# A three-part block kernel: the first expert's weights are loaded during the mixing of attention rows, empty places are left out of the gathers, and two waits of the combination move to their first use

## The chip, the cores and the metric

The kernel runs on one core of one Trainium2 chip. The metric is the device time of one execution in microseconds (us). The kernel before was run three times; a separate execution was profiled, and every row below comes from that one.

## What is computed

The program is two network blocks in float32. The first has two layers (DEPTH = 2). Each layer projects its tokens to queries, keys and values, does attention, mixes the result through an output matrix, applies a layer norm, and then sends each token to a mixture of 32 experts. Layer 0 works on 768 tokens (512 latent, 256 context), layer 1 on the 512 latent ones. The part that matters here, in short (4 groups of 8 experts, 1024 to 512 to 1024 columns):

```python
g_idx = argmax(h @ w_group + b_group)
top_v, top_i = lax.top_k(e_logits[group], 2)
weights = softmax(g_logits)[g_idx] * softmax(top_v)
y_e = (silu(x_e @ w1[e]) * (x_e @ w3[e])) @ w2[e]
out = sum over the token's two experts of weight * y_e
h = layer_norm(ALPHA * h + mods * out, ln_g, ln_b)
```

So layer 0 has 2 x 768 = 1536 assignments of a token to an expert, layer 1 has 1024. All 32 experts' weights are read in each layer: w1, w3 and w2 take 2.10 MB each, 6.29 MB an expert and 201.3 MB a layer. The second block (a recurrent, a convolutional and a dilated branch, gates and a feed-forward part) follows; only its first step, which also finishes the first block, is touched.

## The kernel before

The program is a list of phases, each closed by a barrier of all engines (`program`, L2844). For each layer: `projection_phase`, `attention_phase` (L747), `routing_phase` (L1328), `expert_phase` (L1548). Then `combine_turn_phase` (L1699) and the second block.

**Attention.** qT, kT and V lie in SBUF from the projection to the end of the attention. After the last score tile is weighed (L983), TensorE mixes the rows tile by tile through wout (L998), VectorE makes the layer norm (L1255 to L1273), and the router's logits are made (L1014). SyncE (SP) issues all plain transfers, in the order in which they are written: in this stretch it stores the rows f and h of each tile (L889, L891) and fetches a later tile's (L895).

**Routing.** The routing phase turns the logits into tables. The rows of an expert are cut into units of 32 places (UNIT), at least one unit for each expert. `unit_end` says where each expert's units end, `gather_at` which row of f belongs in each place, `scatter_at` where its result goes. An empty place has row 0 in `gather_at` (L1540), and a number beyond the end, BIG, in `scatter_at` (L1541 to L1545). The experts are put in a sequence: experts 0, 1 and 2 first (EARLY_SLOTS = 3), then the others by their number of rows, in the pattern middle, next below the middle, largest, smallest (L1389 to L1393), so that large and small ones alternate. SP loads the weights of the three early experts in this phase (L1400).

**Experts.** There are four slots for weights (SLOTS = 4), and the load for place i of the sequence goes to slot i modulo 4. The fourth slot's memory is free only once the routing is over. The SP program is this loop (L1588); `load_gate` fetches w1 and w3 in two transfers (L1319), `load_down` w2 in one (L1325):

```python
for i in range(EARLY_SLOTS, NE):
    e = sp.value_load(unit_end[0:1, NE + 1 + i:NE + 2 + i], min_val=0, max_val=NE - 1)
    done = end_of(sp, i - SLOTS) if i >= SLOTS else None
    if i >= SLOTS:
        sp.wait_ge(hidden, done)
    load_gate(sp, g, l, i, e)
    if i >= SLOTS:
        sp.wait_ge(multiplied, done)
    load_down(sp, g, l, i, e)
```

TensorE walks through the sequence. For a unit it multiplies the turned rows xT by w1 and w3 (64 matmuls, L1648), then, after ScalarE's silu (L1667) and VectorE's product and turn (L1684, L1686), by w2 (32 matmuls, L1655). GpSimd (POOL) gathers the rows of the units ahead by an indirect transfer of 128 x 1 KB (L1607), and scatters each result (L1612). The signal `hidden` counts units after L1648, `multiplied` after L1655.

The units of the 32 places of the sequence follow from the inputs. They were counted with the reference's own routing, and agree with the unit boundaries that the trace shows. Layer 0 (64 units): 1 1 1 2 1 7 1 2 1 5 1 2 1 4 1 2 1 4 1 3 1 3 1 3 1 3 1 3 1 3 1 1. Layer 1 (54 units): 3 1 4 1 1 4 1 1 1 3 1 2 1 3 1 2 1 3 1 2 1 2 1 2 1 2 1 2 1 2 1 1. Expert 3 has 5 rows (one unit) in layer 0, and 107 rows (four units) in layer 1.

**Combination.** `combine_turn_phase` works on four tiles of rows. SP fetches, in this order (L1729 to L1740): three 0.52 MB pieces of tile 0 and the gate row; three pieces of tile 1, a 2.10 MB weight block (`load_weights` 1, L1924), the layer norm's two rows (lrow, 0.52 MB each) and gcol; three pieces of tile 2 and another 2.10 MB block; then tile 3. ScalarE weighs the first piece of a tile (L1775), VectorE adds the second and the residual (L1818 to L1825), ScalarE takes the root and norms (L1779, L1781), and VectorE applies lrow (`complete`, L1835). Two waits stand ahead of the loops: ScalarE's for gcol (L1798) and VectorE's for lrow (L1849).

## Time and profile before

| | |
|---|---|
| Median of three runs | 3466.02 us (3466.01 to 3468.59) |
| The profiled execution's own time | 3463.67 us |
| Its span, first to last instruction | 3461.9 us |
| Mean granted TensorE clock | 0.944 |
| Busy: PE, DVE, ACT, POOL | 2905.0, 1047.6, 757.6, 511.8 us |
| Moved by transfers | 684.84 MB |

The busy time of an engine is its instructions' time in the span; "PEclk" is the granted clock as a share of full speed. The page also cuts the span into 40 slices of 86.5 us, with the transfer engines' busy share and GB/s in each. Times inside the trace are counted from the span's start. The layers' expert stretches are the two runs of slices with 422 or 423 GB/s.

### The profile page before, as it was taken

What the parts mean: (1) busy time and instruction counts of PE and PEld (TensorE: products, weight loads), DVE (VectorE), ACT (ScalarE), POOL (GpSimd) and SP (SyncE); (2) the same over time, 40 slices, a digit from 0 to 9 for tenths busy, and PEclk for the clock granted to TensorE, in tenths of its full rate; (3) what the DMA queues carried; (4) which work ended last, traced back from release to release, by engine and by line L of the source; (5) the groups of instructions that cost most, each with busy time, mean ns of one, the idle gap of its engine ahead of it and who ended that gap; (6) DMA issues with size and microseconds to landing.
All of it is one profiled execution on the core that took longest, in us unless ns stands there. A gap on an engine that the chain in (4) does not pass through costs nothing. (4 is left out here: it accounts for less than half of the span.)

```text
span 3461.9 us, 50715 instructions
## 1 busy us (share of the span) xinstructions
PE 2905.0 (84%) x20913; PEld 1617.1 (47%) x20913; DVE 1047.6 (30%) x2201; ACT 757.6 (22%) x1483; POOL 511.8 (15%) x628
## 2 busy tenths in 40 slices
PE   7998888588776698895866652999999999999999
PEld 4555654355444345653534331444444554544444
DVE  3425856311111344754111113443211231211101
ACT  2224641111111323620111112311112220210000
POOL 0003720233332001611322220000000000000000
PEclk8999998799999799996989986999999999999999
DMA  7833002999998552007999996112222112322237
GB/s 296 313 130 114 1 19 106 423 422 423 422 423 368 209 122 96 1 37 294 422 422 422 423 423 244 61 50 81 73 73 73 49 65 79 89 84 87 97 116 260
DMA packets 188525, 684.84 MB, mean 198 GB/s; under 512 B 51438, under 2 KB 92842, under 8 KB 163782
## 3 DMA queue, kind: packets, MB, share of 16 engines
q1 hardware_dynamic: 176550, 655.66, 48.8%
q0 software_dynamic: 11808, 26.78, 2.0%
q8 instruction: 127, 2.08, 0.2%
q14 instruction: 40, 0.33, 0.0%
HBM read 653.89 MB, written 33.98 MB: 199 GB/s over the span
## 5 line engine op out<-in xcount | busy, mean ns | idle before, releaser
L1648 PE MATMUL pH<-w,xT 128*32 128x256 f32 x7552 | 473.5, 406 | 146.4 <-DMA w<-in_moe_w 123.1
L1648 PEld LDWEIGHTS pH<-w,xT 128*32 128x32 f32 x7552 | 295.9, 117 | 305.4 <-issue 179.8
L1655 PE MATMUL pY<-w,hT 128*32 128x256 f32 x3776 | 229.1, 382 | 151.6 <-DVE hT L1686 136.5
L2713 PE MATMUL banks<-hT,wf 128*128 128x512 f32 (+2 forms) x768 | 303.2, 557 | 3.3 <-ACT hT L2770 2.8
L1684 DVE TENSOR_TENSOR hh<-hs,pH 128x128 f32<-128x128 f32 x118 | 33.9, 287 | 807.7 <-ACT hs L1667 807.7
L923 POOL TENSOR_SCALAR E<-E,st 128x768 f32<-128x768 f32 (+3 forms) x80 | 168.3, 2104 | 660.4 <-DVE st L1173 659.8
L1655 PEld LDWEIGHTS pY<-w,hT 128*32 128x32 f32 x3776 | 131.7, 109 | 248.7 <-issue 181.6
L2713 PEld LDWEIGHTS banks<-hT,wf 128*128 128x128 f32 x768 | 140.8, 190 | 164.6 <-issue 154.9
L416 PE MATMUL pa<-aT,w 128*128 128x512 f32 x416 | 206.7, 602 | 1.3 <-DVE aT L680 1.3
L2459 PE MATMUL pa<-hT,ring 128*128 128x512 f32 x384 | 167.8, 592 | 0.0
L2364 PE MATMUL pa<-hT,ring 128*128 128x512 f32 x384 | 165.0, 592 | 1.3 <-PEq L91 1.3
L968 PE MATMUL pT<-ident,E 128*128 128x128 f32 x672 | 112.7, 287 | 55.0 <-ACT PT L1078 31.3
L2752 PE MATMUL banks<-ring,aT 128*128 128x512 f32 x352 | 151.2, 592 | 0.0
L2011 PE MATMUL pa<-hT,ring 128*128 128x512 f32 x320 | 144.2, 607 | 0.0
L998 PE MATMUL pS<-wout,oT 128*128 128x512 f32 x320 | 141.4, 594 | 0.8 <-issue 0.8
L1607 POOL DMA_INDIRECT xg<-f,at_x x124 | 130.2, 1050 | 62.0 <-POOL at_x L1606 58.8
L1612 POOL DMA_INDIRECT y<-y,at_y x122 | 126.1, 1033 | 60.8 <-POOL at_y L1631 59.6
L1667 ACT ACTIVATE hs<-pH 128x128 f32<-128x128 f32 x118 | 32.8, 278 | 466.8 <-PE pH L1648 466.8
L1670 ACT ACTIVATE y<-pY 128x256 f32<-128x256 f32 x118 | 45.4, 385 | 354.8 <-PE pY L1655 354.8
L968 PEld LDWEIGHTS pT<-ident,E 128*128 128x128 f32 x672 | 71.4, 142 | 99.8 <-issue 47.2
L2364 PEld LDWEIGHTS pa<-hT,ring 128*128 128x128 f32 x384 | 72.9, 190 | 93.4 <-issue 93.4
L937 PE MATMUL pS<-kT,qT 64*128 64x256 f32 (+2 forms) x608 | 109.5, 477 | 8.4 <-ACT E L1067 4.9
(468 smaller groups left out, 3653.9 us busy)
## 6 DMA issues: line engine op xcount, KB each, us to landing
w<-in_moe_w SPq DMA_DIRECT2D x192, 2048.0 KB
mw<-in_mod_w SPq DMA_DIRECT2D x24, 2048.0 KB, 16.6
ring<-in_w_ff_down SPq DMA_DIRECT2D x33, 1024.0 KB, 4.8
ring<-in_w_in SPq DMA_DIRECT2D x15, 2048.0 KB, 8.1
ring<-in_w_gate SPq DMA_DIRECT2D x6, 2048.0 KB, 8.6
wf<-in_w_ff_gate SPq DMA_DIRECT2D x11, 1024.0 KB, 5.7
wf<-in_w_ff_up SPq DMA_DIRECT2D x11, 1024.0 KB, 8.1
w<-in_ab_w_in SPq DMA_DIRECT2D x6, 1024.0 KB, 6.5
```

The source lines that it names most:

```text
L416: last = pe.matmul(pa[n % 2][:, 0:512], w[:, i % SLOTS_W, k, tile(c)], aT[:, k, 0:512], start=(k == 0), stop=(k == C - 1))
L923: pool.tensor_scalar(e, e, st[:, u % 4, 6 + b:7 + b], None, ALU.mult).then_inc(readyP, 1)
L968: last = pe.transpose(pT[:, tile(j)], E[:, u % NB, b, tile(i)], ident[:])
L998: last = pe.matmul(pS[n % 2][:, half * 512:(half + 1) * 512], oT[:, k, tile(n)], wout[:, k, half * 512:(half + 1) * 512], start=(k == 4), ...
L1607: pool.indirect_dma_start(out=xg[:, b], out_offset=None, in_=x_rows, in_offset=bass.IndirectOffsetOnAxis(ap=at_x[:, b:b + 1], axis=0), bou ...
L1648: last = pe.matmul(pH[strip(s), 0:2 * P].rearrange("p (j n) -> p j n", j=2), xT[:, k, :], slot_of(g, "w13", b)[:, :, k, s * P:(s + 1) * P] ...
L1655: last = pe.matmul(pY[strip(s), 0:YW], hT[:, k, :], slot_of(g, "w2", b)[:, k, s * YW:(s + 1) * YW], start=(k == 0), stop=(k == HC - 1))
L2011: last = pe.matmul(pa[b][:], ring[:, j % RING, i, tile(c)], hT[:, i, :], start=(i == 0), stop=(i == C - 1))
L2364: last = pe.matmul(pa[b][:], ring[:, j % RING, i, at], hT[:, i, :], start=(i == 0), stop=(i == C - 1))
L2459: last = pe.matmul(pa[b][:], ring[:, j % RING, k, (c % 4) * P:(c % 4 + 1) * P], hT[:, k, :], start=(k == 0), stop=(k == C - 1))
L2713: last = pe.matmul(banks[f % 2][:, j * 512 + cols.start:j * 512 + cols.stop], wf[:, i % 2, j, k, (f % 2) * P:(f % 2 + 1) * P], hT[:, k, co ...
L2752: last = pe.matmul(banks[b][:, h * 512:(h + 1) * 512], aT[:, f, tile(t)], wd[:, m % SLOTS_D, f % 2, h * 512:(h + 1) * 512], start=(f == 0) ...
```

## The change

- One tensor, `room`, now holds qT, kT and V in the attention, and then the weights of expert 0 (w1, w3 and w2). SP waits in the attention phase until the last weighing has begun to leave V alone (`weighed` at its last count), loads expert 0's weights there, and goes on to the stores of f and h.
- The routing phase loads w1 and w3 of experts 1, 2 and 3 and w2 of experts 1 and 2; the expert phase starts with w2 of expert 3. Experts 0 to 3 now lead the sequence, and the other 28 follow in the same pattern. The places then have these units. Layer 0: 1 1 1 1 2 1 7 1 2 1 5 1 2 1 4 1 2 1 4 1 3 1 3 1 3 1 3 1 3 1 3 1. Layer 1: 3 1 4 4 1 1 3 1 1 1 3 1 1 1 3 1 2 1 2 1 2 1 2 1 2 1 2 1 2 1 2 1.
- To make space for w1 and w3 of expert 3, some of the routing's and the experts' tiles lie in what is left of `room` (class `Rest`), where they fit.
- In `gather_at` an empty place now has a number beyond the end, as in `scatter_at`; both gather buffers are set to zero before their first gather.
- In the combination, lrow and gcol are fetched ahead of the 2.10 MB weight block, and the waits for them stand at their first use.

```diff
@@ attention_phase
+            sp.wait_ge(weighed, round_no(U, 0))
+            load_gate(sp, g, l, 0, 0)
+            load_down(sp, g, l, 0, 0)
             for n in range(total):
                 sp.wait_ge(f_ready, n + 1)

-SLOTS, EARLY_SLOTS = 4, 3
+SLOTS = 4
+EARLY = {"w13": 4, "w2": 3}

@@ routing_phase
-            for e in range(EARLY_SLOTS):
+            for e in range(1, SLOTS):
                 load_gate(sp, g, l, e, e)
-                load_down(sp, g, l, e, e)
+                if e < EARLY["w2"]:
+                    load_down(sp, g, l, e, e)
...
-            step(dve.memset(gather_at[:, NU:NU + 3], 0))
+            step(dve.memset(gather_at[:, NU:NU + 3], BIG))
             dve.wait_ge(slot_used, 2 * nt)
             step(dve.tensor_copy(table[:].rearrange("p a w -> p (a w)"), pV[:, :]))
-            dve.tensor_scalar(gather_at[:, 0:NU], table[:, 0], float(STRIPS), strip[:], ALU.mult, ALU.add)
             dve.tensor_scalar(table[:, 1], table[:, 1], -float(BIG), float(BIG), ALU.mult, ALU.add)
             step(dve.tensor_tensor(table[:, 2], table[:, 0], table[:, 2], ALU.add))
-            step(dve.scalar_tensor_tensor(out=table[:, 2], in0=table[:, 2], scalar=float(STRIPS), in1=table[:, 1], op0=ALU.mult, op1=ALU.add))
-            step(dve.tensor_scalar(table[:, 2], table[:, 2], strip[:], None, ALU.add))
-            step(dve.tensor_copy(scatter_at[:, 0:NU], table[:, 2]))
+            for j in (0, 2):
+                last = dve.scalar_tensor_tensor(out=table[:, j], in0=table[:, j], scalar=float(STRIPS), in1=table[:, 1], op0=ALU.mult, op1=ALU.add)
+            step(last)
+            dve.tensor_scalar(gather_at[:, 0:NU], table[:, 0], strip[:], None, ALU.add)
+            step(dve.tensor_scalar(scatter_at[:, 0:NU], table[:, 2], strip[:], None, ALU.add))

@@ expert_phase, sync
-            for i in range(EARLY_SLOTS, NE):
+            for i in range(EARLY["w2"], SLOTS):
+                load_down(sp, g, l, i, i)
+            for i in range(SLOTS, NE):
                 e = sp.value_load(unit_end[0:1, NE + 1 + i:NE + 2 + i], min_val=0, max_val=NE - 1)
...
+                sp.wait_ge(hidden, done)
                 load_gate(sp, g, l, i, e)
...
+                sp.wait_ge(multiplied, done)
                 load_down(sp, g, l, i, e)
@@ expert_phase, gpsimd
             for b in range(2):
+                step(pool.memset(xg[:, b], 0.0))
                 gather(b, b)

@@ combine_turn_phase
                 if t == 1:
-                    load_weights(sp, g, 1)
                     for i, x in enumerate((g["ln_g"], g["ln_b"])):
                         sp.dma_start(lrow[:, i], x[l, 1:2, :].broadcast_to([P, D])).then_inc(lrow_in, 16)
                     sp.dma_start(gcol[:], gain[0].rearrange("(p k) -> p k", p=P)).then_inc(gcol_in, 16)
+                    load_weights(sp, g, 1)
...
             def move(t):
                 act.wait_ge(turned, t + 1)
+                if t == 0:
+                    act.wait_ge(gcol_in, 16)
...
-            act.wait_ge(gcol_in, 16)
...
             def complete(t):
                 dve.wait_ge(n_ready, t + 1)
+                if t == 0:
+                    dve.wait_ge(lrow_in, 32)
...
-            dve.wait_ge(lrow_in, 32)

@@ program
+                nq = TOK if l < DEPTH - 1 else LAT
+                parts = [(C, nq), (6, TOK), (NTILE, 640)]
+                room = keep("room", [P, sum(a * b for a, b in parts)])
+                g["w13"] = [room[:, 0:W13].rearrange("p (j k n) -> p j k n", j=2, k=C)]
+                g["w2"] = [room[:, W13:W13 + W2].rearrange("p (k n) -> p k n", n=D)]
```

## Rows read from the trace of the kernel before

**Rows 1.** The page: GB/s by slice; the scatters.

```profile
GB/s 296 313 130 114 1 19 106 423 422 423 422 423 368 209 122 96 1 37 294 422 422 422 423 423 244 61 50 81 73 73 73 49 65 79 89 84 87 97 116 260
...
L1612 POOL DMA_INDIRECT y<-y,at_y x122 | 126.1, 1033 | 60.8 <-POOL at_y L1631 59.6
```

**Rows 2.** By stretch: PE, PEld, DVE, ACT, POOL busy; clock, transfer share, GB/s.

```profile
480.00:506.00 26.00, 23.78 (x86) 11.55 (x84) 9.71 (x30) 5.12 (x10) 1.20 (x1) 1.00 0.00 1
600.00:1114.00 514.00, 367.79 (x6082) 235.93 (x6082) 104.65 (x325) 83.20 (x160) 162.84 (x272) 0.92 1.01 421
1160.00:1180.00 20.00, 20.00 (x78) 11.80 (x77) 12.73 (x21) 11.59 (x24) 0.00 (x0) 0.93 0.95 342
1508.00:1530.00 22.00, 21.29 (x63) 9.92 (x64) 5.65 (x8) 2.01 (x4) 0.00 (x0) 1.00 0.00 1
1588.00:2096.00 508.00, 323.58 (x5122) 197.23 (x5126) 86.94 (x277) 70.17 (x135) 138.60 (x232) 0.87 1.00 420
```

**Rows 3.** Timeline of PE, experts: start, duration, line [idle time before].

```profile
643.67 5.49 PE L1648 MATMUL pH<-w,xT 128*32 128x256 f32 x64 [11.73 <-DVE xT L1676]
...
652.14 3.66 PE L1648 MATMUL pH<-w,xT 128*32 128x256 f32 x64
...
658.76 3.66 PE L1648 MATMUL pH<-w,xT 128*32 128x256 f32 x64
...
1082.86 6.04 PE L1648 MATMUL pH<-w,xT 128*32 128x256 f32 x64 [5.55 <-DMA w<-in_moe_w]
...
1114.57 5.35 PE L1648 MATMUL pH<-w,xT 128*32 128x256 f32 x64 [2.61 <-DMA w<-in_moe_w]
1121.16 1.93 PE L1655 MATMUL pY<-w,hT 128*32 128x256 f32 x32 [1.24 <-DVE hT L1686]
...
2095.53 6.58 PE L1648 MATMUL pH<-w,xT 128*32 128x256 f32 x64 [8.75 <-DMA w<-in_moe_w]
2103.36 1.93 PE L1655 MATMUL pY<-w,hT 128*32 128x256 f32 x32 [1.25 <-DVE hT L1686]
```

**Rows 4.** Timeline of SP: start us, us to issue, line.

```profile
508.51 0.33 SPq L889 DMA_DIRECT2D f<-f  x1
...
598.90 0.91 SPq L1319 DMA_DIRECT2D w<-in_moe_w  x2
...
649.37 0.81 SPq L1319 DMA_DIRECT2D w<-in_moe_w  x2
...
1645.52 0.83 SPq L1319 DMA_DIRECT2D w<-in_moe_w  x2
...
1678.64 0.83 SPq L1319 DMA_DIRECT2D w<-in_moe_w  x2
```

**Rows 5.** Queues, 600 to 1114 us: packets, MB, engines' share.

```profile
q0 software_dynamic: 6216, 14.86, 7.5%
q8 instruction: 25, 0.41, 0.3%
```

**Rows 6.** Queues, 1588 to 2096 us.

```profile
q0 software_dynamic: 5328, 11.55, 5.9%
```

**Rows 7.** Transfers of the whole span: line, number, KB each, us to landing.

```profile
f<-f SPq DMA_DIRECT2D x10, 512.0 KB, 2.6
```

**Rows 8.** Timelines of PE at the end of the attention and of POOL.

```profile
484.14 1.10 PE L998 MATMUL pS<-wout,oT 128*128 128x512 f32 x2 [0.41 <-issue]
...
638.16 0.52 POOL L1618 MEMSET y<- 128x512 f32 x1
```

**Rows 9.** Timelines of DVE and ACT in the combination.

```profile
2131.39 0.21 DVE L1825 BATCH_NORM_AGGREGATE mv<-bn 128x2 f32<-128x12 f32 x1
2138.45 1.29 DVE L1818 SCALAR_TENSOR_TENSOR y<-y,share 128x1024 f32<-128x1024 f32 x1 [6.85 <-DMA lrow<-in_ln_b]
...
2146.36 1.28 DVE L1818 SCALAR_TENSOR_TENSOR y<-y,share 128x1024 f32<-128x1024 f32 x1
...
2142.34 1.15 ACT L1775 ACTIVATE y<-y,share 128x1024 f32<-128x1024 f32 x1 [0.93 <-DMA y<-h_mid]
```

More of the change, by code:

```diff
@@ L1310, in slot_of, with __init__, sb @@
 def slot_of(g, name, b):
-    return g[name][b] if b < EARLY_SLOTS else g["late_" + name][b - EARLY_SLOTS]
+    return g[name][b]
+class Rest:
+    def __init__(self, room):
+        self.room, self.at = room, W13 + W2
+    def sb(self, ph, name, shape):
+        n = math.prod(shape[1:])
+        if self.at + n > self.room.shape[1]:
+            return ph.sb(name, shape)
+        x = self.room[:, self.at:self.at + n]
+        self.at += n
+        if len(shape) == 3:
+            return x.rearrange("p (a b) -> p a b", a=shape[1])
+        return x.rearrange("p (a b c) -> p a b c", a=shape[1], b=shape[2]) if len(shape) == 4 else x
 def load_gate(sp, g, l, i, e):
@@ L1325, in load_down, with routing_phase @@
     sp.dma_start(slot_of(g, "w2", b)[:], g["moe_w2"][l, ds(e, 1)].rearrange("a (p k) n -> p (a k) n", p=P)).then_inc(g["w2_in"][b], 16)
-def routing_phase(nc, g, l, nt, logits, share, gather_at, scatter_at, unit_end):
+def routing_phase(nc, g, l, nt, logits, share, gather_at, scatter_at, unit_end, rest):
     T = nt * P
@@ L1385, in _ @@
             step(pool.tensor_copy(key[:, NE:NE + 1], token[0:NE, 0:1]))
-            step(pool.tensor_scalar(tie[:], key[:], -1.0, float(EARLY_SLOTS), ALU.mult, ALU.add))
+            step(pool.tensor_scalar(tie[:], key[:], -1.0, float(SLOTS), ALU.mult, ALU.add))
             step(pool.tensor_scalar(tie[:], tie[:], 0.0, 2.0 ** 17, ALU.max, ALU.mult))
@@ L1389, in _ @@
             step(pool.tensor_copy(rank_at[:], count[0:NE, 0:NE]))
-            n = (NE - EARLY_SLOTS) // 4
-            quarters = rank_at[:, EARLY_SLOTS:EARLY_SLOTS + 4 * n].rearrange("p (j q) -> p q j", q=4)
+            n = (NE - SLOTS) // 4
+            quarters = rank_at[:, SLOTS:SLOTS + 4 * n].rearrange("p (j q) -> p q j", q=4)
             for q, (sign, first_rank) in enumerate(((-1.0, 2 * n - 1), (1.0, 2 * n), (1.0, 0), (1.0, 3 * n))):
-                pool.tensor_scalar(quarters[:, q], count[0:NE, 0:n], sign, float(EARLY_SLOTS + first_rank), ALU.mult, ALU.add).then_inc(tabled, 1)
+                pool.tensor_scalar(quarters[:, q], count[0:NE, 0:n], sign, float(SLOTS + first_rank), ALU.mult, ALU.add).then_inc(tabled, 1)
         @block.sync
@@ L1561, in expert_phase @@
         at_y = ph.sb("at_y", [P, 2], I32)
-        xg = ph.sb("xg", [P, 2, XW])
-        xT = ph.sb("xT", [P, C, UNIT])
+        xg = rest.sb(ph, "xg", [P, 2, XW])
+        xT = rest.sb(ph, "xT", [P, C, UNIT])
         hs = ph.sb("hs", [P, P])
@@ L2873, in program @@
                 with ExitStack() as mixer:
-                    qT, kT, V = (keep(n, s, stack=mixer) for n, s in (
-                        ("qT", [P, 8, TOK if l < DEPTH - 1 else LAT]), ("kT", [P, 6, TOK]), ("V", [P, NTILE, 640])))
+                    at = [sum(a * b for a, b in parts[:i]) for i in range(4)]
+                    qT, kT, V = (room[:, at[i]:at[i + 1]].rearrange("p (a b) -> p a b", a=parts[i][0]) for i in range(3))
                     bias = keep("na_bias", [P, 8, 14, HD], stack=mixer) if l == 1 else None
```

32 lines of the change are left out of this document (14 added, 18 removed).

## The prediction

> **What bounds the kernel now.** I read the slices first. Two runs of slices stand at 422 or 423 GB/s, one for each layer's experts [rows 1]. The stretches confirm it: from 600 to 1114 us and from 1588 to 2096 us the transfer engines are busy all the time (share 1.01 and 1.00, 421 and 420 GB/s), while PE is busy for 368 of 514 and 324 of 508 us [rows 2]. One expert's 6.29 MB take 6.29/0.421 = 14.9 us (9.9 for w1 and w3, 5.0 for w2). A unit takes PE 658.76 - 652.14 = 6.62 us [rows 3], so layer 0 has 64 x 6.62 = 424 us of units and layer 1 54 x 6.62 = 357 us, beside 32 x 14.9 = 477 us of weights. PE waits: the 30th place's first unit began after 5.55 us of waiting for weights, the 32nd's after 2.61 us in layer 0 and 8.75 us in layer 1 [rows 3]. So each expert phase is set by transfers, up to the landing of the last weights, and then by the units behind them.
>
> Two facts decide what moved bytes are worth. A load for place i needs the slot of place i - 4, so the load for place 4 (counting from 0) was issued at 649.37 and 1645.52 us, when the first expert's units were through w1 and w3 [rows 4]. And the indirect queue moved 14.86 MB in layer 0 [rows 5]: 66 gathers of 0.131 MB are 8.65, the 1536 real rows of the scatters (4096 B each) 6.29, together 14.94. In layer 1, 56 gathers (7.34) and 1024 rows (4.19) give 11.53 against 11.55 [rows 6]. So today empty places are moved by gathers, and not by scatters, whose empty places are numbered beyond the end.
>
> **Part 1, expert 0 ahead of its phase.** Its three transfers would be issued at about 484 us, when the mixing begins [rows 8], into engines with share 0.00 to 506 us [rows 2], and need 14.9 us, to about 501. The first store behind them on SP comes at 508.51 [rows 4], and the stretch from 1508 to 1530 us is as empty [rows 2]. Cover: that idle time; were it gone, stores and row loads would be late by what is left of the stream. I take 0 (late stores would cost up to 15; nothing can be gained). The wait for `weighed` has only those stores and row loads queued behind it, and passes before they are due.
>
> The Trainium skill, DMA: Bandwidth & Descriptors (Queues, rings and completion order), says that descriptors of one queue are taken in ring order on each engine, which speaks against putting 6.29 MB ahead of small stores. By it a store issued at 490 us would land some 11 us late; the trace has none before 508.51 [rows 4].
>
> Then the ledger of the transfer engines, layer by layer.
>
> Layer 0. Off: 14.9 us (expert 0) and the empty places of the gathers, (8.65 - 6.29)/0.421 = 5.6 us. New: a hole. A transfer starts some 1.3 us after its issue: a lone 0.52 MB store takes 2.6 us to land [rows 7], 1.25 of them its bytes. The phase's own early loads are 18.9 MB, 44.8 us from 598.9 + 1.3 = 600.2 [rows 4], with 0.9 us of gathers among them, so they end at 645.9. The next load still waits for place 0's unit: 649.4 + 1.3 = 650.7, a hole of 4.8 us. The 32nd place's w1, w3 land at 1114.6 - 20.5 + 4.8 = 1098.9. But the end is no longer there: the 31st place, 15.5 us ahead (14.9 and two units' rows), lands at 1083.4 and now has three units, the 32nd one. PE, which has waited, needs 4 x 6.62 and 1.9 for a first unit at the low clock (5.35 to 6.04 us against 3.66 [rows 3]) = 28.4, so it ends at 1111.8; its 32nd place is due at 1105, when the weights are there. Before, PE ended at 1121.16 + 1.93 = 1123.1 [rows 3]. **-11 us.** Bounds: -14 (hole closed by an earlier gather) and -8 (hole 2 us longer, rows worth half).
>
> Layer 1. Off: 14.9 and (7.34 - 4.19)/0.420 = 7.5 us. New holes, larger ones, because expert 0 has three units and expert 3, now fourth, has four. (a) The early loads start at about 1589.5 (the stretch from 1588 is full [rows 2]) and end 44.8 + 0.7 us on, at 1635; the next starts at 1645.5 + 1.3 = 1646.8: 11.8 us. (b) Places 4 and 5 take 29.9 us and some 2 us of rows, to 1679; place 6 may start at 1678.6 + 1.3 = 1679.9 [rows 4]: 1 us. (c) It ends at about 1696. Place 7 waits for expert 3's fourth unit, the twelfth: 1645.3 + 9 x 6.62 = 1704.9, plus 1.3: 10 us. Rows moved inside the holes give back 1.7. Sum of holes 21; the 32nd place lands at 2095.5 - 22.4 + 21 = 2094, the 31st 15.4 earlier, at 2078.7. It has two units: 3 x 6.62 + 1.9 = 21.8, end at 2100.5 against 2103.36 + 1.93 = 2105.3 [rows 3]. **-5 us.** Bounds: -8, and +1 (each hole 2 us longer).
>
> **Part 2, smaller edits.** The two clears of a gather buffer stand before the first gather: half of the 0.52 us that y's clear takes [rows 8] each, with their waits 0.3 to 0.5 us until PE starts; hidden in layer 1 by holes that begin with PE, 0.3 in layer 0, inside the bounds. A scatter, which skips its empty places today, costs POOL 1033 ns [rows 1]; a gather that skips them is taken to cost no more, and POOL is busy for 163 of 514 us [rows 2]: 0. The table's last steps are seven instructions before and after: 0.
>
> **Part 3, the combination.** VectorE was ready at 2131.6 and went on at 2138.45, after 6.85 us of waiting for lrow [rows 9]. Without the 2.10 MB block ahead, lrow lands 5.0 us earlier, and with the wait at its first use neither lrow nor gcol stops the second tile. From 2131.6, the add, the factors, the residual and `complete` take as long as between 2138.45 and 2146.36 [rows 9], 7.9 us, and the root's wait (a table load) about 1 us more: 2140.6. Late next is the third tile: its rows were on hand at 2142.34 [rows 9], and the same bytes stand ahead of them. So its add begins at 2142.34 + 1.15 = 2143.5, not 2146.36. **-2.9 us.** Bounds: 0 (its rows later) and -6.85 (the whole wait).
>
> **Sum.** -11 - 5 - 2.9 = -18.9. The profiled execution took 3463.67 us, 1.8 more than its span; this gives 3444.8. The median of the runs shown is 2.35 us above that execution, so I predict 3466.0 - 18.9 = 3447.1 us. The bounds together give -29 to -7.
>
> The Trainium skill's same page (Specifications) puts memory's limit at about 358 GB/s for a core. By that an expert would take 17.6 us and layer 0 would gain some 3 us more; the trace disagrees, with 421 GB/s over 514 us [rows 2].
>
> **The rivals.** *Skipped rows give nothing (B).* For it: a gather is issued and signalled whatever it moves. Against it: the scatters' skipped rows are missing from the queue's bytes [rows 5, 6], and the queue holds 7.5% of engine time for 6.9% of the bytes [rows 2, 5], so its bytes do cost. The landings of the 31st places come 5.4 and 7.3 us later: -6, +2 and -2.9 are -7, or 3459.
>
> *No holes (C).* If the engines stay full, layer 0 gains 11 + 5 and layer 1 5 + 21, with 2.9: -45, or 3421. For it: they never were idle before [rows 2]. Against it: the slot rule and the issue at 1645.52 [rows 4].
>
> *Slower (D).* The 6.29 MB stream lies beside the mixing, straight-line code whose instructions come through the same transfer engines (0.41 MB of them in the experts' loops alone [rows 5]). If engines starve while it runs, two streams cost up to 2 x 14.9 = 29.8 us: 3477. It decides the sign once more than 18.9/29.8, 63%, of the stream's time is lost. Against it: from 1160 to 1180 us PE is busy for 20.00 of 20 us at a transfer share of 0.95 [rows 2].
>
> *The load isn't early (E).* If `weighed` reached its count only with the last tile mixed, expert 0's 14.9 us would be back in the phase, and layer 0's hole closed: -1 there. In layer 1 they would fill the holes (a) and (b): still -5. Sum -9, or 3457. The count is reached when the last tile's weighing begins, just before 484 us [rows 8], so I give it little.
>
> **How the numbers follow.** Forecast 0.78, B 0.11, C 0.04, D 0.03, E 0.04. The forecast's own range by its bounds is 3437 to 3459; all bounds seldom meet at one end, so it also holds E and half of B, and 8 in 10 need no more: 3437 to 3459. About 0.2%, 6.9 us, is what a measurement of this kernel can tell from no change. Faster: the forecast, C, half of B, which lies at that border, and E less its slow half, 0.78 + 0.04 + 0.055 + 0.02 = 0.90, less 0.02 for the forecast's slow end, 0.88; same: the rest of these, 0.09; slower: D, 0.03.
>
> **What would show it.** Right: three transfers of moe_w issued near 484 and 1510 us; the indirect queue at about 12.6 MB in layer 0 and 8.4 in layer 1; the transfer rate low for 5 us before 650 in layer 0, and for 12 us near 1630 and 10 us near 1690 in layer 1 (on its shifted clock); PE's last expert wait at the 31st place; no wait for lrow or gcol. Wrong: mixing longer than before (D), no holes (C), queue bytes as before or bytes gone and landings unmoved (B). The sum fails above all if a slot frees later than I have it.

## The result, and the profile after

The changed kernel takes 3446.57 us (median of five runs, 3441.95 to 3452.31), the kernel before 3466.02; the ratio is 0.9944, with a 95% interval of 0.9931 to 0.9957. The profiled execution took 3446.33 us for a span of 3444.5 us, 17.4 less than the span before. 3447.1 us was predicted.

**The page of the changed kernel**: GB/s in 40 slices, and the two large queues.

```profile
GB/s 296 312 135 115 1 92 93 398 426 426 426 425 304 220 113 96 1 110 256 367 423 423 424 423 239 58 50 82 73 73 73 49 74 83 82 86 80 98 119 259
...
q1 hardware_dynamic: 176550, 655.66, 49.0%
q0 software_dynamic: 11808, 21.03, 1.6%
```

Against [rows 1], the slice of the mixing (the sixth) now holds 92 GB/s where 19 stood, and the one at 1508 us 110 where 37 stood: the early loads. The indirect queue q0 has 21.03 MB. Between 600 and 1114 us it moved 12.60 MB, from 1578 to 2080 us 8.25; 12.6 and 8.4 were forecast. And the full slices of layer 0 stand at 425 and 426, where [rows 1] have 422 and 423.

**The same kernel by stretch**: length, busy time of PE, PEld, DVE, ACT, POOL (instructions), granted clock, transfer share, GB/s.

```profile
480.00:506.00 26.00, 23.78 (x84) 11.55 (x84) 9.73 (x30) 5.11 (x10) 1.14 (x1) 1.00 0.60 243
600.00:1114.00 514.00, 375.98 (x6178) 241.74 (x6178) 105.76 (x328) 83.76 (x162) 165.00 (x277) 0.92 0.96 405
645.00:649.00 4.00, 4.00 (x56) 1.83 (x48) 0.00 (x0) 0.00 (x0) 0.17 (x1) 0.69 0.11 33
1624.00:1636.00 12.00, 10.02 (x184) 6.69 (x175) 1.55 (x5) 2.60 (x5) 4.71 (x7) 1.00 0.27 101
1686.00:1696.00 10.00, 7.64 (x140) 4.95 (x131) 1.93 (x6) 2.15 (x4) 3.66 (x6) 1.00 0.12 43
```

The first line is the cover of part 1: with 243 GB/s beside it PE is busy for 23.78 us of 26, to the hundredth what it was beside nothing [rows 2]. The last three are the forecast holes: the transfer engines are nearly idle for 4 us before place 4's load in layer 0, and for about 10 us twice in layer 1. **SP's timeline** (start, us, line) has what they end with, and the early load, whose last transfer is issued 24 us before the first store:

```profile
484.46 0.43 SPq L1351 DMA_DIRECT2D room<-in_moe_w  x1
508.37 0.33 SPq L895 DMA_DIRECT2D f<-f  x1
...
649.40 0.84 SPq L1345 DMA_DIRECT2D room<-in_moe_w  x2
...
1635.47 0.82 SPq L1345 DMA_DIRECT2D room<-in_moe_w  x2
...
1695.09 0.81 SPq L1345 DMA_DIRECT2D w<-in_moe_w  x2
1698.70 0.33 SPq L1351 DMA_DIRECT2D w<-in_moe_w  x1
1701.71 1.05 SPq L1345 DMA_DIRECT2D room<-in_moe_w  x2
```

**PE's timeline**, same kernel, the ends of the two expert phases (start, duration, line, idle time before):

```profile
1083.33 5.84 PE L1677 MATMUL pH<-w,room 128*32 128x256 f32 x64 [4.81 <-DMA w<-in_moe_w]
...
1110.29 1.93 PE L1684 MATMUL pY<-w,hT 128*32 128x256 f32 x32 [1.24 <-DVE hT L1715]
...
2070.46 5.50 PE L1677 MATMUL pH<-w,room 128*32 128x256 f32 x64 [8.76 <-DMA w<-in_moe_w]
...
2090.47 1.93 PE L1684 MATMUL pY<-w,hT 128*32 128x256 f32 x32 [1.24 <-DVE hT L1715]
```

The 31st place is the last that PE waits for, in both layers; with it PE has four units left in layer 0, three in layer 1 [rows 3]. Layer 0 ends at 1112.2 in place of 1123.1: -10.9 us.

For all later readings the span is cut into four: **A**, layer 0's experts, from the first load of its routing phase (596.96 us here, 597.10 before) to the end of PE's last unit; **M**, from there to layer 1's routing phase; **B**, the same as A for layer 1; **Z**, the rest of the span. In the profiled executions, us:

| kernel | A | M | B | Z | span |
|---|---|---|---|---|---|
| before | 526.0 | 463.2 | 519.0 | 1356.6 | 3461.9 |
| changed | 515.3 | 464.5 | 515.6 | 1352.1 | 3444.5 |
| changed, once more (`again`) | 515.4 | 460.4 | 516.3 | 1350.0 | 3439.0 |

So layer 0 gave -10.7 and layer 1 -3.4 or -2.7. M and Z vary from one execution of the same kernel to the next: over all 14 profiles of this study M takes values from 460.3 to 464.5, and Z has an even wider spread. One stretch of M in the changed kernel's two executions shows a part of the reason (columns as above):

```profile
1337.00:1357.00 20.00, 13.81 (x76) 9.98 (x78) 10.75 (x36) 10.05 (x22) 10.52 (x4) 0.66 0.95 323
```

```profile
1337.00:1357.00 20.00, 13.58 (x116) 10.20 (x116) 13.52 (x45) 11.67 (x27) 11.69 (x5) 0.91 0.95 321
```

The first was granted a clock of 0.66 there and did 76 matmuls in the time in which the second did 116 at 0.91. These two executions differ by 4.2 us in M, where the runs of this kernel lie 10 us apart; how the rest of the spread arises was not looked into. So A and B are read below rather than whole times: A was 515.3, 515.4 and 515.4 us in three executions in which layer 0's experts run the same.

### The profile page after: what moved, and what is told of

Its sections match the earlier page's. It is cut to its first block and busy times, and to the rows that moved or that the text cites. A ratio compares the mean times of both kernels' runs of the same rounds, so it can differ in the third digit from the quotient of the medians.

```text
span 3444.5 us, 50705 instructions
## 1 busy us (share of the span) xinstructions
PE 2907.5 (84%) x20913; PEld 1623.6 (47%) x20913; DVE 1047.9 (30%) x2201; ACT 756.7 (22%) x1483; POOL 512.3 (15%) x632
## 3 DMA queue, kind: packets, MB, share of 16 engines
q0 software_dynamic: 11808, 21.03, 1.6%
## 5 line engine op out<-in xcount | busy, mean ns | idle before, releaser
L1677 PE MATMUL pH<-w,room 128*32 128x256 f32 x5504 | 340.0, 401 | 77.5 <-DMA w<-in_moe_w 77.5
L1677 PEld LDWEIGHTS pH<-w,room 128*32 128x32 f32 x5504 | 217.7, 116 | 184.7 <-issue 110.9
L1684 PE MATMUL pY<-w,hT 128*32 128x256 f32 x2752 | 166.3, 381 | 107.9 <-DVE hT L1715 103.5
L1677 PE MATMUL pH<-room 128*32 128x256 f32 x2048 | 136.1, 424 | 57.7 <-DMA room<-in_moe_w 34.8
L1684 PEld LDWEIGHTS pY<-w,hT 128*32 128x32 f32 x2752 | 96.4, 109 | 177.8 <-issue 134.3
L1677 PEld LDWEIGHTS pH<-room 128*32 128x32 f32 x2048 | 82.0, 122 | 106.7 <-issue 58.4
L943 PE MATMUL pS<-room 64*128 64x256 f32 (+2 forms) x608 | 110.7, 482 | 8.4 <-ACT E L1073 4.9
```

The costliest lines, as they stand in the source:

```text
L1677: last = pe.matmul(pH[strip(s), 0:2 * P].rearrange("p (j n) -> p j n", j=2), xT[:, k, :], slot_of(g, "w13", b)[:, :, k, s * P:(s + 1) * P] ...
L1684: last = pe.matmul(pY[strip(s), 0:YW], hT[:, k, :], slot_of(g, "w2", b)[:, k, s * YW:(s + 1) * YW], start=(k == 0), stop=(k == HC - 1))
```

## The experiments

Twelve kernels ran, in three jobs, each beside the kernel before on the same chip (its medians: 3463.67, 3464.23 and 3466.22 us). Their phases:

| kernel | median, us | ratio, 95% | A | M | B | Z |
|---|---|---|---|---|---|---|
| again | 3444.56 | 0.9945 [0.9932, 0.9958] | 515.4 | 460.4 | 516.3 | 1350.0 |
| gather_all | 3448.20 | 0.9953 [0.9940, 0.9966] | 515.2 | 460.3 | 519.6 | 1352.6 |
| late_first | 3456.81 | 0.9980 [0.9971, 0.9988] | 522.7 | 464.5 | 515.3 | 1352.2 |
| three_early | 3437.72 | 0.9922 [0.9908, 0.9935] | 512.3 | 463.5 | 508.8 | 1355.6 |
| spread | 3436.80 | 0.9923 [0.9909, 0.9936] | 509.6 | 463.9 | 515.0 | 1349.4 |
| spread_all | 3445.15 | 0.9944 [0.9931, 0.9958] | 512.9 | 464.0 | 520.1 | 1354.9 |
| three_spread | 3429.93 | 0.9899 [0.9884, 0.9914] | 508.8 | 460.3 | 506.8 | 1355.1 |
| skip_only | 3457.50 | 0.9979 [0.9969, 0.9989] | 524.0 | 463.3 | 514.7 | 1356.8 |
| stream_mid | 3447.86 | 0.9943 [0.9928, 0.9959] | 515.4 | 464.5 | 515.7 | 1355.8 |
| comb_only | 3461.84 | 0.9991 [0.9982, 1.0000] | 526.4 | 462.2 | 517.8 | 1355.0 |
| room_only | 3457.34 | 0.9975 [0.9964, 0.9985] | 522.2 | 464.5 | 516.2 | 1351.6 |
| three_place | 3426.62 | 0.9882 [0.9867, 0.9897] | 505.1 | 464.5 | 504.9 | 1356.4 |

A, M, B and Z come from one execution of each kernel, the medians from 4 to 11 executions. The two can be held against each other, with the changed kernel's first runs as a thirteenth row. What a median gained on the kernel before in its job, less what A and B gained, is 2.0 to 7.0 us (mean 5.1) in the nine rows with an early load of expert 0, and -0.1 to 3.5 us (mean 1.5) in the four without. So by the medians some 3 to 4 us that go with the early load lie outside A and B. The profiles don't show where: M + Z is 816.4 us on average in the nine and 817.5 in the four. This stays open.

### again: the changed kernel once more

No edit.

> The changed kernel once more, unedited, as the base for the other three. Its phases should stand where they stood: 31st place of layer 0 multiplied at about 1083, last unit ended at about 1112, layer 1's expert phase ended 12 to 13 us earlier than in the kernel before. In the first profile 3.7 us went lost between the two expert phases, and 3.7 us were won in the second block, which the change does not touch. If these two come from the granted clock by chance, this run shows other values there; if the change makes them, it shows the same.

A came back to 0.1 us and B to 0.7. The 3.7 us lost in M did not come back (460.4); Z, 1350.0, was even shorter. So neither is the change's alone, and M's went with the clock of the stretch shown; Z needs the kernels below.

### gather_all: are skipped rows worth anything?

```
-            step(dve.memset(gather_at[:, NU:NU + 3], BIG))
+            step(dve.memset(gather_at[:, NU:NU + 3], 0))
...
-            for j in (0, 2):
-                last = dve.scalar_tensor_tensor(out=table[:, j], in0=table[:, j], scalar=float(STRIPS), in1=table[:, 1], op0=ALU.mult, op1=ALU.add)
-            step(last)
+            dve.tensor_scalar(table[:, 0], table[:, 0], float(STRIPS), None, ALU.mult)
+            step(dve.scalar_tensor_tensor(out=table[:, 2], in0=table[:, 2], scalar=float(STRIPS), in1=table[:, 1], op0=ALU.mult, op1=ALU.add))
```

> Empty places are gathered again (row 0), all else as changed. My theory: a byte of a gather costs the weights the same time as any other, so layer 0 ends 4 to 6 us later and layer 1 6 to 8 us later, 10 to 14 us in all, and the indirect queue moves about 14.9 and 11.5 MB. Rival B (skipped rows give nothing): queue bytes as said, but no landing moves, 0 to 2 us.

Queue q0 between 600 and 1110 us, **with all places gathered**, and PE's start on the 31st place:

```profile
q0 software_dynamic: 6240, 14.86, 7.5%
```

```profile
1085.28 5.01 PE L1676 MATMUL pH<-w,room 128*32 128x256 f32 x52 [4.85 <-DMA w<-in_moe_w]
```

The bytes are back (14.86 MB, as in [rows 5]). This run's routing phase began 1.8 us later than the changed kernel's, and its 31st place 1085.28 - 1083.33 = 1.95 later: **nothing moved in layer 0**; A is 515.2 against 515.3. In layer 1 it is 3.3 to 3.9 us. So neither theory holds: the bytes cost about half their mean price in layer 1 and nothing in layer 0.

### late_first: expert 0 loaded in the routing phase again

```
-            sp.wait_ge(weighed, round_no(U, 0))
-            load_gate(sp, g, l, 0, 0)
-            load_down(sp, g, l, 0, 0)
...
-            for e in range(1, SLOTS):
+            for e in range(0, SLOTS):
```

> Expert 0's weights are loaded in the routing phase again, first of four, all else as changed. My ledger: layer 0 ends about 10 us later (14.9 us of bytes, less the hole of 4 to 5 us that they fill), layer 1 by 0 to 1 us, since its holes of 9 and 9 us take the 14.9 us up. Rival: holes are no real loss (C), or the early load works in both layers alike, then each layer ends 12 to 15 us later. Rival D (the stream costs the mixing something): the stretch from the stream to the routing phase gets shorter than in the changed kernel in both layers.

A is 7.4 us longer, where about 10 were expected, B 0.3 to 1.0 shorter, where 0 to 1 longer was. The pattern is the ledger's: without the early load the hole of layer 0 is gone (from 645 to 649 us this kernel has a share of 1.03 and 418 GB/s), and in layer 1 the holes eat all that the early load brings. There this kernel still has one hole, behind expert 3's units, of 4.6 us (a share of 0.43 over 8 us), against 18.1 us of two holes in the changed kernel:

```profile
1696.00:1704.00 8.00, 6.76 (x128) 4.65 (x124) 1.22 (x3) 0.68 (x3) 3.33 (x6) 1.00 0.43 131
```

The **31st place of this kernel** begins at 1091.15:

```profile
1091.15 3.66 PE L1674 MATMUL pH<-w,room 128*32 128x256 f32 x64 [2.98 <-DMA w<-in_moe_w]
```

That is 495.6 us after its routing phase began at 595.6, in place of 1083.33 - 596.96 = 486.4: 9.2 us, where 14.9 less a hole of 4.8 say 10.1. Here the first unit's matmuls by w1 and w3 took 3.66 us, there 5.84, and of the 9.2 us 7.4 remain at the end. The medians are further apart than the phases, 3456.81 against 3444.56, 12.3 us; the profiled execution of this kernel was the fastest of its eleven.

### three_early: only three experts fixed in front

```
-EARLY = {"w13": 4, "w2": 3}
+EARLY = 3
...
-            for i in range(EARLY["w2"], SLOTS):
-                load_down(sp, g, l, i, i)
-            for i in range(SLOTS, NE):
+            for i in range(EARLY, NE):
                 e = sp.value_load(unit_end[0:1, NE + 1 + i:NE + 2 + i], min_val=0, max_val=NE - 1)
-                done = end_of(sp, i - SLOTS)
-                sp.wait_ge(hidden, done)
+                done = end_of(sp, i - SLOTS) if i >= SLOTS else None
+                if i >= SLOTS:
+                    sp.wait_ge(hidden, done)
```

(and the same for `multiplied`; the sequence's arithmetic and the routing phase's loads take 3 for 4, as before the change).

> The changed kernel, but only experts 0, 1 and 2 are fixed in front, as before the change; the fourth place goes to the expert that the sequence picks by count, and its weights are loaded when the expert phase starts. In layer 1 this puts a one-unit expert in place of the four units of expert 3. My ledger: layer 0 has one hole of 6 us, ahead of the fourth place's weights instead of 4 to 5 us behind them, and its last place ends about 2 us earlier (more of its units lie inside the covered part); layer 1 keeps the hole near 1630 us (9 to 10 us) and loses the one near 1690 us (9 us), so it ends 6 to 8 us earlier. Sum 8 to 10 us below the changed kernel. Rival: the holes are not what sets layer 1's end, then 0 to 2 us.

A is 3.0 us shorter and B 6.8 to 7.5. **Its stretches** at the times of layer 1's two holes (columns as above):

```profile
1624.00:1636.00 12.00, 9.52 (x176) 6.37 (x171) 2.43 (x6) 2.61 (x5) 4.20 (x8) 1.00 0.41 135
1686.00:1696.00 10.00, 8.76 (x167) 6.12 (x160) 1.22 (x3) 2.33 (x4) 4.44 (x8) 1.00 1.01 422
```

The second hole is closed (43 GB/s in the changed kernel, 422 here), the first still open. So hole (c) of the prediction was a real loss and came from fixing expert 3, with its four units, in the fourth place. That choice costs the change 7 us by the medians (3437.72 against 3444.56 on the same chip), 10 by A and B.

### spread, spread_all: which rows cost

After `gather_all` the question was why 2.26 MB more cost nothing. In the routing of these inputs a unit of 32 places holds 24 real rows on average in layer 0, 19 in layer 1, packed from place 0 up. New placing: place j on partition 4 (j mod 8) + j div 8 of each strip.

```
+            step(dve.tensor_scalar(place_of[:], place_of[:], -8.0, None, ALU.mult))
+            dve.scalar_tensor_tensor(out=place_of[:], in0=count[:], scalar=8.0, in1=place_of[:], op0=ALU.mult, op1=ALU.add)
-            dve.scalar_tensor_tensor(out=place_of[:], in0=place_of[:], scalar=-float(UNIT), in1=count[:], op0=ALU.mult, op1=ALU.add)
...
+            step(dve.tensor_copy(iota_i[:, 0:P], count[:]))
+            step(dve.tensor_scalar(iota_i[:, 0:P], iota_i[:, 0:P], 2, None, ALU.arith_shift_right))
+            step(dve.tensor_copy(slot[:, 0], iota_i[:, 0:P]))
+            step(dve.scalar_tensor_tensor(out=place_of[:], in0=slot[:, 0], scalar=-(UNIT - 1.0), in1=place_of[:], op0=ALU.mult, op1=ALU.add))
```

> The changed kernel with the real rows of a unit put on other partitions: place j of a strip of 32 goes to partition 4*(j mod 8) + j/8 instead of partition j. The rows, the bytes and the units are the same. Why: gathering the empty places again moved 2.26 MB more in layer 0 and no landing later, 2.87 MB more in layer 1 and its end 3.5 us later, where mean rates say 5.4 and 6.8 us. New theory: each transfer engine serves fixed groups of four partitions of a strip, a weight's landing waits for its fullest engine, and places 0 to 3 are real in nearly every unit. From the routing of these inputs, the first group of four carries 253 real rows in layer 0 and 202 in layer 1, and the mean group 192 and 128. At an eighth of 422 GB/s per group, with gather and scatter (8192 bytes for each row), evened rows are worth (253 - 192) x 8192 B / 52.8 GB/s = 9.5 us in layer 0 and 11.5 us in layer 1. So layer 0 should end 7 to 9 us earlier (four more instructions of the routing phase cost up to 1 us), layer 1 8 to 11 us, and the whole 15 to 20 us less than the changed kernel. Rival: the engines take the rows in turns, whatever their partition, and skipped rows cost their descriptor's time: then nothing moves, 0 to 2 us slower. The Trainium skill, DMA: Bandwidth & Descriptors (The descriptor swizzle), states that engine 8 x (partition >> 6) + ((partition >> 2) & 7) writes a partition of a 128-partition transfer, which is the first theory's grouping; no run has shown it here so far.

> The same placing, but empty places are gathered again (row 0). First theory: now every engine carries the same, so the skipping that was worth 0 and 3.5 us without the new placing is worth its mean rate here: this kernel is 5 to 6 us later in layer 0 and 6 to 7.5 us in layer 1 than the spread kernel, 11 to 13 us in all, and still 4 to 8 us faster than the changed kernel, since its scatters are evened. Rival (rows in turns): as the kernel that gathers all places, 0 to 4 us slower than the changed one.

The cleanest measure leaves the phases' starts out: from PE's start on the 8th unit to its start on the 61st in layer 0, on the 21st to the 52nd in layer 1; both ends wait for weights. The ends in layer 0, **spread** and then **spread_all**:

```profile
1078.30 5.10 PE L1682 MATMUL pH<-w,room 128*32 128x256 f32 x64 [3.28 <-DMA w<-in_moe_w]
```

```profile
1079.50 3.80 PE L1681 MATMUL pH<-w,room 128*32 128x256 f32 x36 [4.49 <-DMA w<-in_moe_w]
```

| us | changed | gather_all | spread | spread_all |
|---|---|---|---|---|
| layer 0, 53 units | 388.4 | 388.2 | 382.3 | 384.8 |
| layer 1, 31 units | 312.0 | 315.0 | 309.4 | 313.7 |

In layer 0's 53 units the fullest group of four places has 211 real rows of 212, the fullest after spreading 171. By the fullest group, at 4096 B a row and 52.8 GB/s (an eighth of 422): gathering all costs 1 row or 0.1 us (measured -0.2), spreading wins 40 rows twice, in gather and scatter, or 6.2 us (measured 6.1), and gathering all on top of spreading costs 41 rows or 3.2 us (measured 2.5). Three of three. In layer 1's 31 units (114 rows of 124, 70 after spreading) it says 0.8, 6.8 and 4.2 us; measured are 3.0, 2.6 and 4.3. So there the theory carries the third but not the first two, and what else counts in layer 1 stays open.

That the placing of rows on partitions costs or saves time at the same bytes is shown; that an engine serves fixed partitions is inferred from the fit, since the trace names no engine per transfer. The Trainium skill, DMA: Bandwidth & Descriptors (The descriptor swizzle), gives just this grouping for a whole 128-partition transfer, and layer 0 agrees with it: 0.1, 6.2 and 3.2 us by that grouping, -0.2, 6.1 and 2.5 measured. Layer 1 does not in two of three.

The whole: `spread` is 3436.80 against a changed kernel at 3444.56 in the job before, less than the 15 to 20 expected. Two reasons show: layer 1's stretch gave 2.6 of its 6.8, and the additional instructions of VectorE put off PE's second unit by 0.4 us in layer 0 and 1.9 to 2.5 us in layer 1, where PE's start sets the holes' ends. B fell by 0.7 to 1.3 us only.

### three_spread: both additions

> Both additions on the changed kernel: only three experts fixed in front (6.8 us faster by itself) and the rows on other partitions. First theory: the two act on different things, the idle stretches ahead of place 4 and place 7, and the load of the fullest engine, so their gains add: 20 to 27 us below the changed kernel, less what more idle stretches or PE's own units take back where the weights now land early. If PE's units become the bound, the gain stops short, at 15. Rival (rows in turns): as the three-early kernel.

3429.93 us, 14.6 below the changed kernel's 3444.56: less than the 20 to 27 expected. A is 3.5 us shorter than in `three_early` (5.7 from the changed kernel to `spread`), B 2.0. The likely reason is the later start of PE's second unit, 58.1 - 54.5 = 3.6 us in layer 0 and 51.4 - 48.4 = 3.0 in layer 1 after the routing phase began; `three_place` below tests it.

### skip_only: one part of the change on the kernel before

The table's and the clears' lines of the diff, nothing else.

> The kernel before with one part of the change: empty places are not gathered (with the two clears of the gather buffer). Mean rates would give -5.6 in layer 0 and -7.5 us in layer 1. By the fullest engine it is less: of 66 x 4 = 264 rows of a group in layer 0 253 stay, of 224 in layer 1 202, so 11 and 22 rows x 4096 B / 52.8 GB/s = 0.9 and 1.7 us. I expect -1 in layer 0 and -2 to -4 in layer 1. If it gives 5 and 7, the fullest engine is not the reason that the changed kernel without it lost so little.

A -2.0, B -4.4, time 0.9979 [0.9969, 0.9989], some 7 us. Mean rates say 5.6 and 7.5, the fullest group 0.9 and 1.7, and -1 and -2 to -4 were expected. Both layers lie between the two theories, layer 0 nearer to the fullest group, layer 1 in the middle.

### stream_mid: the early load where the engines are not idle

```
-            sp.wait_ge(weighed, round_no(U, 0))
-            load_gate(sp, g, l, 0, 0)
-            load_down(sp, g, l, 0, 0)
...
                 sp.dma_start(g["h_mid"][tile(n), :], h[:, n % 2]).then_inc(h_stored, 16)
+                if n == 1:
+                    sp.wait_ge(weighed, round_no(U, 0))
+                    load_gate(sp, g, l, 0, 0)
+                    load_down(sp, g, l, 0, 0)
```

> Expert 0's weights are issued in the middle of the mixing, behind the store of the second tile's row and ahead of the load of tile 3's row, instead of before the first store. It tests the cover of part 1: what the load costs where the transfer engines are not idle. My theory: transfers of SP's queue land in the order of issue, so the row load behind it, 3.1 us by itself, lands some 15 us later, at about 544 us in place of 529; tile 3 (its store is issued at 557 us) needs that row near 545 to 550, so the mixing gets 0 to 5 us longer in layer 0, and as much in layer 1. Rival D (the stream slows straight-line code as such): the mixing gets longer by up to 15 us in each layer, and PE's work beside the stream thins out. Rival: the small transfers pass the stream, nothing moves. In the changed kernel the mixing took 88.6 us from the first store to the routing phase, as before.

**SP's timeline in the mixing**, and below it the fastest, the middle and the slowest landing of the transfers that read or write h between 500 and 600 us, of this kernel; then the same line of the changed kernel:

```profile
527.97 1.27 SPq L1346 DMA_DIRECT2D room<-in_moe_w  x2
529.28 0.47 SPq L1352 DMA_DIRECT2D room<-in_moe_w  x1
530.57 0.33 SPq L902 DMA_DIRECT2D h<-in_x  x1
542.06 0.33 SPq L892 DMA_DIRECT2D f<-f  x1
544.45 0.33 SPq L894 DMA_DIRECT2D h_mid<-h  x1
552.33 0.33 SPq L902 DMA_DIRECT2D h<-in_ctx  x1
```

```profile
DMA to landing us min/median/max: 2.6/3.1/19.2
```

```profile
DMA to landing us min/median/max: 2.6/2.6/3.3
```

The row load behind the stream landed 19.2 us after its issue (at 549.8), 16.1 us more than the 3.1 of one by itself, where some 15 more were expected, and the next row load could be issued only at 552.33, 7.9 us after the store ahead of it in place of 2.6. So transfers of one queue do queue up behind 6.29 MB, which take 14.9 us. The Trainium skill, DMA: Bandwidth & Descriptors (Queues, rings and completion order), says that each engine takes the descriptors of a ring in their order, and this trace agrees, with 19.2 us. But the mixing did not notice: from the first store of f to the last it took 81.5 us (510.15 to 591.62), in the changed kernel 81.4 (508.37 to 589.81), and in layer 1 47.4 us in both. Both rivals fall: nothing passes the stream, and straight-line code beside it is not slowed. The cover of part 1 is wider than the prediction needed.

### comb_only: the combination alone

> The kernel before with the combination's part of the change alone. Both expert phases as before. My step: VectorE's wait of 6.85 us for lrow goes, the third tile's rows are late next: 2.9 us. In the changed kernel the phase gained only some 1.3 us up to the third tile, since its rows landed 1.5 us later after the phase's start than before; from the end of layer 1's experts to the end of the program, four kernels with this edit took 1352.1, 1350.0, 1352.6 and 1352.2 us and another 1356.5, where the kernel before and the kernel with skipping alone took 1356.6 and 1356.8. So 2 to 4 us. Rival: nothing here, the shorter ends come from the granted clock: then this kernel takes 1356 or more.

**VectorE and ScalarE** in this kernel's combination (start, duration, line, idle before):

```profile
2132.63 1.28 DVE L1819 SCALAR_TENSOR_TENSOR y<-y,share 128x1024 f32<-128x1024 f32 x1 [0.54 <-ACT y L1775]
...
2144.07 1.28 DVE L1819 SCALAR_TENSOR_TENSOR y<-y,share 128x1024 f32<-128x1024 f32 x1 [3.10 <-ACT y L1775]
...
2142.89 1.15 ACT L1775 ACTIVATE y<-y,share 128x1024 f32<-128x1024 f32 x1 [6.96 <-DMA y<-h_mid]
```

and in the **changed kernel's**:

```profile
2132.88 1.29 DVE L1848 SCALAR_TENSOR_TENSOR y<-y,share 128x1024 f32<-128x1024 f32 x1 [3.06 <-ACT y L1804]
...
2131.70 1.15 ACT L1804 ACTIVATE y<-y,share 128x1024 f32<-128x1024 f32 x1 [6.92 <-DMA y<-h_mid]
```

No wait for lrow is left [rows 9]; late next are the third tile's rows, in both. Counted from the phase's first load (2118.80 before, 2119.0 here, 2106.5 in the changed kernel), the third add comes at 27.6, 25.1 and 26.4 us: -2.5 alone and -1.2 in the changed kernel, whose rows landed at 25.2 in place of 23.9. Z is 1355.0. The twelve profiles with the edit have Z from 1349.4 to 1356.4, mean 1353.4, the two without 1356.6 and 1356.8: some 3 us, with a spread as large. (The 1356.5 of the expectation is `three_early`'s, and too long by 0.9: its last unit ends at 2081.25 us.) The whole kernel's ratio, 0.9991 with an interval up to 1.0000, allows anything from 0 to 6 us.

### room_only: the new places in memory alone

`three_early` with expert 0 loaded in the routing phase and all places gathered; what is left of the change is where the tiles lie (and the two clears of the gather buffer and the combination).

> Only the new places in memory (expert 0's weights, x, the gather buffer and xT where queries, keys and values were) and the combination's edit; expert 0 is loaded in the routing phase, three experts are fixed in front, and empty places are gathered. Why: from 60 to 480 us into layer 0's routing phase the transfer engines are full in every kernel, but they move 422 GB/s in the kernel before and in the one with skipping alone, and 426 GB/s in the changed kernel, in the one with the late first load and in the one with three in front; in 420 us that is 1.7 MB or 4 us. These three share only the new places in memory. If those are the cause: 426 GB/s here, layer 0 3 to 4 us shorter than before (526.0 us from routing to last unit), layer 1 (422 against 423 to 424 GB/s) 0 to 2. Rival (the early load or the order makes it): 422 GB/s and no gain there.

The same 420 us, from 60 to 480 us into layer 0's routing phase, of **the kernel before**, of **room_only** and of the **changed kernel**:

```profile
657.10:1077.10 420.00, 319.33 (x5504) 207.69 (x5504) 69.71 (x172) 74.95 (x143) 140.30 (x230) 0.96 1.01 422
```

```profile
657.50:1077.50 420.00, 322.32 (x5504) 209.10 (x5504) 69.68 (x172) 75.22 (x144) 141.77 (x232) 0.96 1.01 427
```

```profile
657.00:1077.00 420.00, 325.35 (x5576) 212.07 (x5580) 70.94 (x175) 75.51 (x145) 141.84 (x232) 0.97 1.01 426
```

The share is 1.01 in all three and the rate 1% apart. A is 3.8 us shorter than before (4.2 against `comb_only`), B 2.9 (1.6 against `comb_only`). **The new places alone are worth that**, with no byte less.

### three_place: the best version

`three_spread`, with the table of places loaded as a constant instead of worked out:

```
+            sp.dma_start(place_of[:], g["place_of"]).then_inc(place_in, 16)
             for e in range(1, EARLY):
...
-            step(dve.tensor_copy(place_of[:], iota_i[:, 0:P]))
-            dve.scalar_tensor_tensor(out=place_of[:], in0=place_of[:], scalar=-float(UNIT), in1=count[:], op0=ALU.mult, op1=ALU.add)
...
+            dve.wait_ge(place_in, 16)
             for i in range(2 * nt):
...
+    k["place_of"] = np.tile((np.arange(P) % 4 * 8 + np.arange(P) % UNIT // 4).astype(f), (P, 1))
```

> The kernel with three in front and the rows spread over the partitions, but the table of places is a constant that is loaded, and not worked out by VectorE: six of its instructions are gone from the routing phase, where the spread kernels' expert phase began 0.6 to 2.6 us later in layer 0 and 1.8 to 2.4 us later in layer 1. PE's first unit sets both idle stretches, so each layer should end 1.5 to 3 us earlier: 2 to 5 us below the spread kernel with three in front, 3425 to 3428 us. Rival: the later start was not VectorE's, 0 to 1 us.

3426.62 us, ratio 0.9882 [0.9867, 0.9897] to the kernel before, twice the gain of the change. PE's second unit begins 54.4 and 48.2 us after the routing phase's first load, as in `three_early`, and A is 3.7 us shorter than in `three_spread`, B 2.0: the late start was VectorE's. The gain on the kernel before on the same chip grows from 34.3 to 39.6 us, by 5.3. Against `three_early`, which differs from it in the places of the rows and in where their table comes from, A is 7.2 us and B 4.0 shorter.

## Why the prediction was right, and where it was not

**The total** was 0.5 us off, the two layers' terms -11 and -5 for a measured -10.7 and -3 (-3.4, -2.7). The mechanism holds: transfers set both phases, the early load comes free, and in layer 1 the holes take it back. But layer 0's number is right by errors that cancel, and so is the total: -11 and -5 and -2.9 were measured as -10.7, about -3 and -1.2, together some 15 of the medians' 19.45 us. The other 4 are no term of the prediction; that they made up for its misses is luck.

- *Part 1 costs nothing*: right. It is issued at 483.61 and done before the first store; `stream_mid` shows that even a row load that landed 19.2 us after its issue was covered. D falls by this run as by the busy time of the mixing; E falls by the time of issue.
- *Layer 0, early load and hole*: mechanism right. Predicted 14.9 less 4.8 at the landing, that is 10.1; measured 9.2 at the 31st place and 7.4 at the end of PE's units. The medians give 12.3, and the 3 to 4 us beside A and B that go with the early load are open.
- *Layer 0, rows, -5.6*: **wrong**. The step that failed is "the empty places of the gathers, (8.65 - 6.29)/0.421", bytes divided by the mean rate of 16 engines. The 31st place lands no later when all are gathered, and skipping alone, in the kernel before, gave 2.0. What was cut were bytes of the late places of a unit, and what counts, by the fit of `spread` in this layer, are places 0 to 3, real in almost every one. The argument against rival B, that the queue's share of engine time is in proportion to its bytes, is true of the mean and says nothing of the fullest engine.
- *Layer 0, what made up for it*: a term that the prediction did not have, the new places in memory, -3.8.
- *Layer 0, the tail*: right. The 31st place was to land at 1083.4 and PE began at 1083.33; the end was to be at 1111.8 and came at 1112.2; no wait for the 32nd. So even this landing, right to 0.1 us, came from a sum with two wrong terms in it.
- *Layer 1, holes*: right in place, and in size within 3 us. (a) and (c) were forecast at 11.8 and 10 us less 1.7 for rows, from 1635 and from 1696 us; on this kernel's clock, 9.5 us earlier, that is 1625 and 1686, where they lie. Stretches of 4 us add up to 9.1 and 9.0 us of idle engines (layer 0: 4.9, for 4.8); the 1 us of (b) does not show. They take up the early load entirely: `late_first` has B 0.3 to 1.0 us shorter. `three_early` shows that (c) was avoidable, at 7 us. That the same four fixed experts cost the kernel without the early load 4.6 us of idle engines was not in the prediction.
- *Layer 1, rows, -7.5*: half wrong, by the same step: 3.3 to 3.9 by `gather_all`, 4.4 by `skip_only`. Here too the places in memory (-1.6 to -2.9) fill a gap. The fullest group explains 0.8 of the 3.0 us that `gather_all` cost over 31 units of this layer; the rest stays open.
- *The change in three steps*, whose sum is the whole by their making. From the kernel before to `room_only` (places) to `late_first` (skipping, and four experts fixed in front) to the changed kernel (early load), A goes -3.8, +0.5, -7.4, sum -10.7, and B -2.9, -0.8, +0.3, sum -3.4. The second step is small because the fourth fixed expert works against the skipping. `three_early` prices it at 3.0 and 6.8 us beside the early load; without that, layer 1 has its hole of 4.6 us against the 4.4 of `skip_only`. The split between the two in this step was not measured by itself.
- *Combination, -2.9*: mechanism and next wait right. -2.5 by itself, -1.2 in the changed kernel, whose rows landed 1.3 us later; why they did is open.
- *What is left*: 17.4 us of span less 10.7, 3.4 and 1.2 leaves 2.1, out of M (+1.3) and Z's remainder (-3.3). Those are the size of the differences between two executions of one kernel (M 4.2, Z 2.1), and were no part of the forecast.

Rival B, at 0.11, was nearer to the truth than its chance: its premise holds in layer 0 and half of it in layer 1. Its time, 3459, was wrong: it had neither the memory places nor what the medians gained outside the two phases.

On the bandwidth, the prediction set 421 GB/s against the Trainium skill's 358 for a core (DMA: Bandwidth & Descriptors, Specifications). Another page of the Trainium skill, HBM Reference (Specifications (TRN2)), says that 358 is the share when both cores of a pair stream, and that a core alone reaches about 425. With that sentence there is no contradiction: this kernel runs on one core, and the 420 to 427 GB/s here are that case.

## What to carry to other kernels

Bytes divided by the mean rate may misprice a transfer that lies on few partitions more than on others. The gathers of this kernel fill from partition 0 up; in such a case ask which partitions are always in use, and try interleaving the places before cutting bytes: 6.1 us of layer 0's 53 units here, 2.6 of layer 1's 31, from the order alone. A load moved ahead is worth its time less the hole that opens where the next one waits for its slot, so put pieces with little work into the first slots. And where two executions of the same kernel differ by as much as the term in question, cut the span into phases at events that the edit cannot touch, and compare those; then hold their sum against the medians, which here showed 3 to 4 us that the phases had not.

## What the runs showed of the hardware that was not expected

- The same transfers at a share of 1.01 moved 422 GB/s with the tiles in their old places in memory and 426 or 427 with expert 0's weights, x and xT where queries, keys and values had been (layer 0, from 60 to 480 us after the routing phase began; in layer 1, from 130 to 480 us, 422 or 423 against 424). Of the 14 profiles, three have the old places and eleven the new ones, with no exception in either layer. What it is in the places was not tried.
- A share of 1.01 says that the engines have work on average, not that none of them is the last: between the changed kernel and `spread`, which both show 1.01, 6 us of 388 were to be had by moving rows to other partitions.
- Of 14 executions M lay at 460.3 or 460.4 us in three and at 462.2 to 464.5 in eleven. In the 20 us that begin 225 us after layer 0's last unit, the three had a granted clock of 0.91, and so had two of the eleven, with M at 462.2 and 463.2; the other nine had 0.66, with M from 463.3 up. The three load expert 0 early, as six of the others do.
